# Last chunk of a two-layer block with experts: the convolution's taps spread over 36 ticks in place of 29, and the work behind them moved five or seven ticks later

## The reference, cut to what matters

```
h = rmsnorm(x);  p_conv, p_attn, p_ssm = split(h @ w_in)
y_conv = silu(layernorm(causal_conv_31_taps(val * sigmoid(gate))))
y_attn = stick_breaking_attention(q, k, v);  y_ssm = s5_scan(p_ssm), gated
x = x + concat(rmsnorm(y_conv), rmsnorm(y_attn), rmsnorm(y_ssm)) @ w_out
x = x + softmax(rmsnorm(x) @ w_mq . memory keys) . memory values @ w_mo
h = rmsnorm(x);  q = h @ peer_wq              # 8 heads
scores = q . sub_keys                         # 2 x 128 for each head
16 best of the 16 x 16 sums of the best keys  # 16 experts for each row and head
x = x + sum over the 128 experts of softmax(best) * gelu(u_e . h) * v_e
```

## Time and profile before

| | us |
|---|---|
| median of three executions | 1709.49 (1709.29 to 1709.78) |
| the profiled execution's own time | 1710.15 |
| its span, first to last instruction | 1708.2 |
| TensorE busy | 1560.3 (91%) |
| VectorE busy | 1213.6 (71%) |
| ScalarE busy | 608.8 (36%) |
| GpSimd busy | 590.1 (35%) |
| DMA: moved, mean rate over the span | 675.16 MB, 395 GB/s |
| share of the chain that ended last: TensorE, DMA, VectorE | 48%, 33%, 12% |

### The profile page before, as it was taken

One profiled execution on the slowest core, in us unless ns is written; L12 is line 12 of the kernel. 1 busy time (PEld: TensorE's weight loads), 2 busy tenths in 40 slices (PEclk: granted clock), 3 DMA queues, 4 the chain that ended last, 5 costly groups with the idle time before them and its releaser, 6 DMA issues.

```text
span 1708.2 us, 19646 instructions
## 1 busy us (share of the span) xinstructions
PE 1560.3 (91%) x6618; PEld 945.5 (55%) x6618; DVE 1213.6 (71%) x3359; ACT 608.8 (36%) x1461; POOL 590.1 (35%) x527
## 2 busy tenths in 40 slices
PE   9999899899999999989998889989999999777776
PEld 8877775447557777544645446545656554222232
DVE  7821799985887658897555677996666777667665
ACT  4142432553345133265232242354333223222222
POOL 0000343443334323354332442343333444433331
PEclk9999999999999999999999999999999999999999
DMA  9654999999999999999999999999999999999996
GB/s 386 250 197 154 365 421 421 416 414 421 421 420 401 420 418 416 420 420 422 421 422 421 422 420 421 399 404 407 421 407 418 421 421 421 422 421 422 421 421 257
DMA packets 93860, 675.16 MB, mean 395 GB/s; under 512 B 10408, under 2 KB 10688, under 8 KB 12224
## 3 DMA queue, kind: packets, MB, share of 16 engines
q0 software_dynamic: 73728, 536.90, 75.9%
q1 hardware_dynamic: 20032, 137.00, 19.8%
HBM read 672.81 MB, written 1.05 MB: 394 GB/s over the span
## 4 chain that ended last, share of the span: by engine, by line
PE 48%; DMA 33%; DVE 12%; ACT 4%; issue 2%; POOL 0%; SPq 0%; DVEq 0%; POOLq 0%
DMA slots<-expert_rows,expert 32%; PE bank L934 21%; PE bank L444 10%; DVE slots L1899 5%; PE bank L627 4%; PE bank L922 3%; PE bank L919 3%; ACT diag L1427 1%; DVE sg L1466 1%; DMA slots<-w_blocks 1%; PE bank L715 1%; PE bank L452 1%; ACT L1440 1%; PE bank L694 1%; DVE htok L1750 1%
## 5 line engine op out<-in xcount | busy, mean ns | idle before, releaser
L934 PE MATMUL bank<-slots,diag 128*128 128x512 f32 x1916 | 903.9, 608 | 122.4 <-ACT diag L1427 119.1
L1059 POOL DMA_INDIRECT slots<-expert_rows,expert x512 | 588.2, 1149 | 1093.0 <-PE bank L934 866.7
L1899 DVE CUSTOM_DVE_ANT_0 slots<-slots,htok 128x1024 f32<-128x1024 f32 x512 | 625.3, 1222 | 272.9 <-DMA slots<-expert_rows,expert 271.4
L934 PEld LDWEIGHTS bank<-slots,diag 128*128 128x128 f32 x1916 | 347.8, 192 | 530.9 <-issue 320.7
L1440 ACT ACTIVATE gel<-dot 128x2 f32<-128x2 f32 (+1 forms) x258 | 52.4, 203 | 599.4 <-DVE dot L1899 598.6
L1427 ACT ACTIVATE diag<-ident,coef 128x128 f32<-128x128 f32 x479 | 168.3, 395 | 196.0 <-DVE coef L1466 194.8
L444 PEld LDWEIGHTS bank<-hT,ring 128*128 128x128 f32 x1552 | 187.5, 192 | 42.4 <-issue 39.8
L444 PE MATMUL bank<-hT,ring 128*128 128x128 f32 x1552 | 188.5, 275 | 2.0 <-DMA ring<-w_blocks 1.2
L1466 DVE SCALAR_TENSOR_TENSOR coef<-gel,ginv,gexp 128x2 f32<-128x2 f32 (+1 forms) x258 | 54.6, 212 | 96.3 <-ACT gel L1440 95.0
L1440 ACT ACT_TABLE_LOAD x68 | 87.2, 1283 | 1.2
L1466 DVE SCALAR_TENSOR_TENSOR sg<-pad,prm,sg 128x128 f32<-128x128 f32 x240 | 71.4, 341 | 0.0
(11 more groups left out here) (333 smaller groups left out, 1558.4 us busy)
## 6 DMA issues: line engine op xcount, KB each, us to landing
ring<-w_blocks SPq DMA_DIRECT2D x92, 1024.0 KB, 9.4
slots<-w_blocks SPq DMA_DIRECT2D x22, 1024.0 KB, 14.0
slots<-expert_rows,expert POOLq DMA_INDIRECT x512, 15.4
kept<-w_blocks SPq DMA_DIRECT2D x4, 1024.0 KB, 12.3
keys<-w_blocks SPq DMA_DIRECT2D x2, 1024.0 KB, 11.1
kv<-w_blocks SPq DMA_DIRECT2D x2, 1024.0 KB, 14.1
prm<-small SPq DMA_DIRECT2D x2, 768.0 KB, 13.3
x<-x_rows SPq DMA_DIRECT2D x2, 512.0 KB, 10.9
```

Source lines behind the costliest of these rows:

```text
L934: last = mm(bank[h][:, :], diag[:, i % DIAGS, :], slots[:, n % SLOTS, D + h * 512:D + (h + 1) * 512], start=m == 0, stop=n == end)
L1059: nc.gpsimd.indirect_dma_start(slots[:, n % SLOTS, :], None, experts_d, bass.IndirectOffsetOnAxis(ap=idx[q % 2][:, k:k + 1], axis=0),).the ...
L1899: v.tensor_tensor_reduce(out=slots[:, s, 0:D], in0=slots[:, s, 0:D], in1=htok[:, ph % 2, :], scale=1.0, scalar=0.0, op0=ALU.mult, op1=ALU.add,
```

## The change

It touches chunk 3 alone. The convolution's 62 instructions are spread over 36 ticks (14 to 49), where they had 29 (14 to 42). What follows them (transposes, mean and variance, roots, silu, the convolution's sum and its root) comes seven ticks later; the chain's two transposes go to banks 5 and 6, where both went to bank 4. The two sums of attention and scan stay at tick 51 and their root at 52, the convolution's sum goes to 58 and its root to 59. All that hangs on `LATER` comes five ticks later: w_out at 51 to 61, `mixed` at 58, 60 and 62, w_mq at 69 to 79, the attention over the memory at 75 to 88, w_mo at 83 to 93, the add to x at 94, the norm for the experts at 95 to 97. The heads' queries come five ticks later for the first two (99, 103) and four for the rest (110, 118, and on by 8). "Late x" goes from ticks 51 and 52 to 53 and 54.

Late heads and routes keep their ticks. So TensorE now takes W7 (tick 87) before M2 (89) and M3 (92), and the blocks' order becomes O1, head 5's, O2, O3, O0, head 6's, Q0 to Q3, M0, M1, W7, M2, M3, W0, W1, W2. Head 5's block, which had been put in front of O3, is put right behind O1, since O3 is taken after it now (the change of `behind`). W7 is last used at tick 100, and with the new order it lies in the place of `ring` that W0 takes next.

```diff
-LATER = [0] + [5] * (NST - 1)
+LATER = [0, 5, 5, 10]
+CONV_LATER = [0, 0, 0, 7]
...
-         [94 + 4 * i for i in range(5)], [94, 98] + [106 + 8 * i for i in range(6)]]
+         [94 + 4 * i for i in range(5)], [99, 103] + [110 + 8 * i for i in range(6)]]
...
             def conv(ci):
-                at = BEGIN[ci]
+                at = BEGIN[ci] + CONV_LATER[ci]
+                bt, bn = (5, 6) if CONV_LATER[ci] else (4, 4)
                 yield at + (43 if ci else 40)
...
-                yield at + (51 if ci else 47)
+                yield at + CONV_LATER[ci] + (51 if ci else 47)
                 fill(7, ("conv sum", ci))
...
                     if turned_anew(ci, h):
-                        yield at + tick - 4
+                        yield at + tick - 2
...
-                    behind = max(k for k in range(j) if order[k] == (l, first))
-                    issue.insert(issue.index(behind), j)
+                    opens = max(k for k in range(j) if order[k] == (l, 0))
+                    behind = [k for k in range(opens, j) if order[k] == (l, first)]
+                    issue.insert(issue.index(behind[-1]) if behind else issue.index(j - 1) + 1, j)
...
-                yield at + (52 if ci else 48)
+                yield at + CONV_LATER[ci] + (52 if ci else 48)
                 name = ("conv sum", ci)
...
-                    yield at + 14 + n * (29 if ci else 25) // (CT * TAPS)
+                    yield at + 14 + n * ((29 if ci else 25) + CONV_LATER[ci]) // (CT * TAPS)
...
-                for i, (first, tick) in enumerate(((2, 53), (6, 55), (0, 57)) if ci else ((2, 49), (6, 50), (0, 52))):
-                    yield at + tick
+                for i, (first, tick) in enumerate(((2, 48), (6, 50), (0, 52)) if ci else ((2, 49), (6, 50), (0, 52))):
+                    yield at + LATER[ci] + tick
```

More of the change, by code:

```diff
@@ L537, in conv @@
             def conv(ci):
-                at = BEGIN[ci]
+                at = BEGIN[ci] + CONV_LATER[ci]
+                bt, bn = (5, 6) if CONV_LATER[ci] else (4, 4)
                 yield at + (43 if ci else 40)
                 eng.wait_ge(conv_ready, ci + 1)
-                fill(4, ("conv t", ci))
+                fill(bt, ("conv t", ci))
                 for i in range(CT):
-                    last = nc.tensor.transpose(bank[4][:, i * P:(i + 1) * P], cacc[:, i, :], ident[:, :])
-                last.then_inc(filled[4], 1)
+                    last = nc.tensor.transpose(bank[bt][:, i * P:(i + 1) * P], cacc[:, i, :], ident[:, :])
+                last.then_inc(filled[bt], 1)
                 yield at + (48 if ci else 44)
                 read_out(("conv t", ci))
-                fill(4, ("conv n", ci))
+                fill(bn, ("conv n", ci))
                 for i in range(CT):
-                    last = nc.tensor.transpose(bank[4][:, i * P:(i + 1) * P], lnt[:, i, :], ident[:, :])
-                last.then_inc(filled[4], 1)
+                    last = nc.tensor.transpose(bank[bn][:, i * P:(i + 1) * P], lnt[:, i, :], ident[:, :])
+                last.then_inc(filled[bn], 1)
             def attention(ci):
@@ L1330, in late_queries @@
                     if turned_anew(ci, h):
-                        yield at + tick - 3
+                        yield at + tick - 1
                         if late_home(ci, h) is hT:
@@ L1726, in conv @@
                     ins.then_inc(conv_step if n < CT * TAPS - 1 else conv_ready, 1)
-                yield at + (44 if ci else 41)
+                yield at + CONV_LATER[ci] + (44 if ci else 41)
                 name = ("conv t", ci)
@@ L1731, in conv @@
                 v.bn_aggr(lnmv[:, :], lnst[:, :]).then_inc(conv_var, 1)
-                yield at + (47 if ci else 43)
+                yield at + CONV_LATER[ci] + (47 if ci else 43)
                 eng.wait_ge(conv_root, ci + 1)
```

## The result

The changed kernel takes 1715.53 us (median of six executions, 1713.85 to 1717.45), beside 1710.01 us for the kernel before in six executions of the same kind: **slower by 0.3%, ratio 1.003 with a 95% interval of 1.002 to 1.004**. The profiled execution is the fastest of the six, at 1713.85 us with a span of 1711.9, so its trace shows 3.7 us of the 5.5.

The account below looks back on a forecast made before the run. DMA was taken to bound the kernel. Terms -1.5 + 1.5 - 0.8 + 1.0 - 1.0 + 2.5 summed to +1.7 us: 1711.9 us for a profiled execution, 1711.2 for the median; 8-in-10 range 1705.0 to 1717.5.

Parts of the forecast that it names:

- no change: Whole kernel: idle DMA time goes in some stretches and comes back in others; 1708 to 1713 us, chance 0.46.
- my bound of 0.2%: Whole kernel: about 0.2% (3.4 us) is what a measurement can tell from no change.
- slower: Rival: W7's ring place keeps W0 to W2 away until tick 100 while norm and route meet; 1714.5 us, chance 0.30.
- Bound: Whole kernel: DMA sets the time, mostly at 421 GB/s; chunk 3's idle DMA time allows at most 7.6 us gain.
- (f): Ticks 94 to 98: add and norm meet head 7's route with gathers alone; 2.5 us lost, bounds nothing and 6.
- my allowance of 3 us: Chunk 3: compute may owe 3 us, as the nine slots fill up, before DMA idles.
- (a): Before tick 43: fewer taps, O2 held behind head 5's block; gain 1.5 us, bounds nothing and 3.7.
- (b): Behind tick 41: more taps with no weights in flight; 1.5 us lost, bounds nothing and 3.5.
- (c): Late x, moved to tick 53: its 2.57 us wait for ScalarE's root goes; gain 0.8 us, bounds nothing and 1.3.
- (d): Ticks 61 to 65: the mixing shares them with head 5's route; 1.0 us lost, bounds nothing and 4.
- (e): At 1250 to 1262 us: memory attention mostly passes head 6's route; gain 1.0 us, bounds 1.5 gain, 0.5 loss.
- (g): Tick 103: TensorE waits some 4 us for W0; priced at nothing with three blocks in flight, else up to 3.

Follow-up runs that it names:

- hold alone: Kernel before, with W0 taking W7's place in the ring and W1, W2 the two behind, nothing else of the change: 1713.14 us against 1709.35, ratio 1.0022.
- second profile of either code: Ticks 23 to 58 profiled again in kernels sharing that code: old code, hold alone (ratio 1.0022); new code, changed kernel with W0 to W2 one ring place further (1.0002).
- experiment 5: Block issues shifted to fill ticks 28 to 36: O3 earlier, O1 and O2 later (two), on the kernel before; O2 and O3 earlier on experiment 1. Ratios 1.0000 to 1.0005.
- experiment 1: Changed kernel with W0, W1 and W2 one place further in the ring: 1709.59 us against 1708.97 for the kernel before, ratio 1.0002.
- experiments 5 and 6: Kernel before with O3 earlier, O1 and O2 later (two kernels), late x two ticks later, or late x and O1, O2 later together: ratios 0.9999 to 1.0001.
- taps over 29 ticks: Changed kernel with the convolution's taps over 29 ticks as before, all that hangs on LATER still five ticks later: 1713.8 us, ratio 1.0032 to the kernel before.
- O2 in front: Changed kernel with O2 issued in front of head 5's block, SyncE's old order: 1714.96 us, ratio 1.0038 to the kernel before.

## Why the prediction was right and where it was not

I gave 1711.2 us, 1705.0 to 1717.5, with no change as likeliest. The time is inside the range and my bound of 0.2% is passed, so it is the rival **slower** that came about, by the mechanism that I had named for it: W7's place keeps W0 to W2 away until tick 100. What I had called likeliest, 1711.2 and no change that can be told, did not come. Of the terms one was too small by more than half, and the small ones in front of tick 58 are below what one profile can show, so where they agree with it that is partly luck.

- **Bound.** Right: from 1385 to 1685 us the changed kernel runs at 421 GB/s as the one before, and the time is lost where DMA is not full, in chunk 3.
- **(f)** is the mis-sized term. I took 2.5 us lost for ticks 94 to 98; measured are 6.5 us more than before over ticks 85 to 103. The step that failed is where I let the stretch start: at tick 94, with ticks 89 to 93 level with DMA, since the add and the norm had left them. Ticks 85 to 94 alone lost 3.1 us. Ticks 89 to 94 still took 18.2 us, TensorE busy in all of it: W7's products and head 7's keys stood there before as well (1281.7, 1286.9 and 1292.2), and products of M2 and M3 had taken the place of what left. And ScalarE, in its fixed order, waited for those products with the next gelu behind it, as VectorE's timeline of the changed kernel shows:

```profile
1280.20:1298.40 18.20, 18.20 (x70) 10.29 (x69) 7.46 (x21) 2.64 (x10) 5.43 (x5) 1.00 0.95 363
1298.40:1316.00 17.60, 17.23 (x58) 8.63 (x57) 14.25 (x44) 10.43 (x19) 8.23 (x7) 1.00 0.94 345
```

```profile
1287.21 0.22 DVE L1471 SCALAR_TENSOR_TENSOR coef<-gel,ginv,gexp 128x2 f32<-128x2 f32 x1 [5.80 <-ACT gel L1445]
...
1294.59 0.22 DVE L1471 SCALAR_TENSOR_TENSOR coef<-gel,ginv,gexp 128x2 f32<-128x2 f32 x1 [4.86 <-ACT gel L1445]
```

  ScalarE's own waits there, for head 7's query and its scores:

```profile
1286.70 0.38 ACT L1347 ACTIVATE qT<-bank 128x256 f32<-128x256 f32 x1 [6.41 <-PE bank L447]
...
1294.08 0.38 ACT L1352 ACTIVATE scores<-bank 128x256 f32<-128x256 f32 x1 [5.92 <-PE bank L887]
```

  So ticks 89 to 94 owed 5.8 us against five gathers, and 2.5 of them were lost: my allowance of 3 us was spent here, and I counted it once more behind tick 94. There the sum came out better: 17.6 us of compute, put at 19, owe 5.2, and 3.2 were lost, so the second count was wrong by no more than 1 us. The hold was 32 us long, from M3's landing at 1290.2 to W0's issue, and I had priced only a part of it.

  One reading behind the rival was wrong as well. "A whole route with one block in flight" at 1300 to 1312 was a route with almost none: W2 was issued at 1307.99, and from 1296 to 1311 the kernel before moved no weights at all. The gathers kept the DMA engines busy all the same:

```profile
1296.00:1311.00 15.00, 15.00 (x66) 9.15 (x65) 12.43 (x43) 6.10 (x15) 6.18 (x6) 1.00 1.01 410
```

  So a route by itself does without weights (0.4 us lost in ticks 94 to 99 before, 1.1 with the hold alone). Norm and route together don't (3.2 us in ticks 94 to 99 of the changed kernel), nor do W7's products with those of w_mo (2.5 us in ticks 89 to 94).
- **(a)** isn't borne out. I took a gain of 1.5 us; ticks 23 to 41 lost 4.4 against 3.9 (3.2 and 4.3 in the second profile of either code). "Ssm y" came 1.7 us sooner (head 5's block issued at 1110.10) and not 3.3. The three blocks were issued on end before 1111, but the rate of ticks 29 to 36, which was to rise above 360, was 334, and 344 before:

```profile
1095.90:1115.60 19.70, 19.70 (x105) 11.06 (x102) 19.62 (x54) 9.94 (x19) 9.35 (x7) 1.00 0.92 334
```

  The step behind it failed: I treated a better fill of this stretch as time won. In the four kernels of experiment 5 it isn't.
- **(b) and (c)** together were put at 0.7 us lost and read 0.9 (ticks 41 to 58, 2.4 against 1.5), but the second profiles have 3.1 against 3.3, so this agreement proves nothing. The dip that I had named ahead of O0's issue is there in the changed kernel (359 GB/s from 1158.6 to 1165.3) and not in that of experiment 1 (423 in the same ticks, 50 to 53). "Late x" no longer waits: TensorE's timeline of the changed kernel has it straight behind O1's product.

```profile
1165.80 1.88 PE L631 MATMUL bank<-ring,hT 128*128 128x512 f32 x4
1167.52 1.04 PE L869 MATMUL bank<-ident,htok 128*128 128x128 f32 x8
```

  The convolution's roots did as priced: the one of the variance (`lnroot`) now shares a table load with that of the two sums, and the one of its own sum (L1227) needs another, so the group of the gelu's table loads (L1440 before) has 69 where there were 68. ScalarE's timeline of the changed kernel:

```profile
1162.98 0.40 ACT L1432 ACTIVATE diag<-ident,coef 128x128 f32<-128x128 f32 x1 [1.06 <-DVE coef L1471]
1163.40 1.28 ACT L1224 ACT_TABLE_LOAD   x1
1164.69 0.26 ACT L1224 ACTIVATE groot<-bank,epsb 128x2 f32<-128x2 f32 x1
1164.85 0.29 ACT L1149 ACTIVATE lnroot<-lnmv,epsb 128x1 f32<-128x1 f32 x1
...
1182.16 1.28 ACT L1227 ACT_TABLE_LOAD   x1
1184.74 0.26 ACT L1227 ACTIVATE groot<-bank,epsb 128x1 f32<-128x1 f32 x1 [1.30 <-PE bank L622]
```

  The load begins 0.02 us behind the activation before it, and the next activation 0.01 us behind the load, so the switch costs 1.3 us. The Trainium skill (page "ScalarE: Activation LUTs", section "What ACT_TABLE_LOAD costs") adds a drain of 1.38 us to each switch; no row here shows it, and the measurement decides.
- **(d)** was put at 1.0 and is nothing: 420 to 424 GB/s through ticks 58 to 77, with five blocks of weights (O0, head 6's, Q0, Q1 and Q2, issued from 1167.71 to 1195.59) beside the mixing and the route.
- **(e)** agrees: 1.0 gained by my count, 1.3 read from the table in ticks 77 to 85 (422 GB/s from 1250 to 1262). It isn't shown, though: the five kernels that experiments 5 and 6 made of the kernel before leave these ticks as they were, and lose from 0.1 to 1.6 us in ticks 77 to 85.
- **(g)** was right in mechanism, and in price for this kernel. TensorE waits for W0, and its products then run at the lower of the clock's two levels for a while (3.46 us for sixteen records that take 1.95 else; granted clock 0.55 in these 3.5 us), but with three blocks in flight DMA stays at 421:

```profile
1331.13 3.46 PE L447 MATMUL bank<-hT,ring 128*128 128x128 f32 x16 [3.69 <-DMA ring<-w_blocks]
```

```profile
1331.10:1334.60 3.50, 3.46 (x17) 3.50 (x18) 0.00 (x0) 0.00 (x0) 0.00 (x0) 0.55 1.00 421
```

  In other kernels with the hold ticks 103 to 125 lose 0.2 us (taps over 29 ticks), 1.2 (hold alone) and 2.0 (O2 in front), inside the 3 that I had named.
- **The chances.** 0.46 for no change leaned on seven small terms that were to cancel, and 0.30 for slower on the one with the widest bound (nothing to 6 us). With (f) at its upper bound the sum is +5.2 and the forecast 1714.7.

## What to carry to other kernels

Where DMA bounds a kernel and transfers are held by a few places used in turn, look up after every reordering how long each block stays in its place and what stands behind it in the queue: here one block used twice, three places and one queue made a change of ticks cost 5 us, and taking other places took it back. Time that DMA loses in a stretch set by compute is not won by moving transfers into it: check first whether the stretch itself gets shorter. Before a difference of a microsecond between two profiles is explained, see by how much two profiles of the same code differ in that stretch: it was up to 2.2 us here. And an allowance, such as the slots that may fill up before DMA idles, can be spent only once between two points where compute is level with DMA.

## What the runs showed of the hardware beyond that

A load of 1 MB took 9 to 10 us to land alone beside the gathers, but three issued within 1.3 us landed about 5 us apart (1318.6, 1323.6 and 1328.5 in the kernel with the hold alone). Gathers and blocks together moved 417 GB/s in that time (1309.0 to 1328.5), no more than elsewhere: a burst after a hold can't make up for what was lost before it, since the rate doesn't rise above that of a full DMA.

```profile
1309.00:1328.50 19.50, 15.17 (x59) 9.73 (x58) 10.67 (x28) 6.64 (x16) 4.43 (x5) 0.91 1.00 417
```

Gathers alone can fill DMA too (410 GB/s at a busy share of 1.01 from 1296 to 1311, 421 GB/s in the 300 us behind chunk 3), as long as slots come free in time. The kernel before had medians of 1710.01, 1708.97, 1709.35 and 1709.41 us in the four sets of runs, so times of different sets are compared by their ratios only.
